# A two-layer hybrid decoder trunk: TensorE's wait before it reuses an accumulator counts finished tiles instead of first sums

## What is computed

```python
for i in range(2):
    h = rms_norm(x, norm_mix_pre[i])
    z = h @ w_in[i]                        # 2048 x 6400
    y_r = rwkv7_mix(token_shift(z[:, :3328]), ...)   # 16 heads of 64, delta-rule state
    y_a = moba_attention(rope(q), rope(k), v)        # 8 heads of 128
    y = concatenate([y_r, y_a]) @ w_out[i]           # 2048 x 2048
    x = x + rms_norm(y, norm_mix_post[i])
    h = rms_norm(x, norm_mlp_pre[i])
    m = square(relu(h @ w_up[i])) @ w_down[i]        # 2048 x 8192, 8192 x 2048
    x = x + rms_norm(m, norm_mlp_post[i])
```

## Time and profile before

| | |
|---|---|
| median of 3 runs | 2776.0 us (2775.13 to 2776.6) |
| the profiled execution | 2776.0 us, of which the span of the engines' work is 2774.3 us |
| PE busy | 97% of the span |
| DVE busy | 64% |
| ACT busy | 44% |
| POOL busy | 9% |
| mean granted TensorE clock | 0.988 of full speed |

### The profile page before, as it was taken

How to read it: one execution, slowest core, us unless ns; L and a number is a source line. 1 busy time by engine, 2 the same in 40 slices (tenths; PEclk the granted TensorE clock), 3 DMA queues, 4 the chain that set the end, 5 groups by cost and what they waited for, 6 DMA issues and landing times.

```text
span 2774.3 us, 50423 instructions
## 1 busy us (share of the span) xinstructions
PE 2682.2 (97%) x16787; PEld 2197.0 (79%) x16787; DVE 1775.2 (64%) x2961; ACT 1219.9 (44%) x1976; POOL 244.9 (9%) x341
## 2 busy tenths in 40 slices
PE   7999999999999999999989999999999999999998
PEld 6777777777888888888877777777778888888886
DVE  5777776655756656556577777777566566565565
ACT  5444443345544434444454444444454344444443
POOL 3211111100000000000012222221000000000000
PEclk9999999999999999999999999999999999999999
DMA  6333333345566565565633333332455665555654
GB/s 196 97 93 93 101 99 100 93 141 170 182 198 189 188 192 180 196 188 189 190 112 102 100 100 93 100 93 94 158 169 187 198 187 190 183 188 198 188 186 155
DMA packets 438043, 420.25 MB, mean 151 GB/s; under 512 B 19518, under 2 KB 351952, under 8 KB 437968
## 3 DMA queue, kind: packets, MB, share of 16 engines
q1 hardware_dynamic: 434320, 412.75, 47.5%
q0 software_dynamic: 3648, 6.52, 0.9%
HBM read 417.10 MB, written 2.10 MB: 151 GB/s over the span
## 4 chain that ended last, share of the span: by engine, by line
PE 90%; DVE 6%; issue 1%; ACT 1%; DMA 0%; DVEq 0%; POOL 0%; SPq 0%; ACTq 0%; POOLq 0%
PE gemm_bank L516 29%; PE gemm_bank L517 15%; PE gemm_bank L541 11%; PE gemm_bank L543 10%; PE gemm_bank L542 10%; PE gemm_bank L519 2%; PE mix_bank L696 2%; DVE b_zt L1157 1%; PE mix_bank L708 1%; PE mix_bank L705 1%; PE mix_bank L660 1%; DVE b_rn L1251 1%; PE mix_bank L726 1%; PE mix_bank L730 1%; PE mix_bank L740 1%
## 5 line engine op out<-in xcount | busy, mean ns | idle before, releaser
L516 PE MATMUL gemm_bank<-b_hT,b_whi 128*128 128x512 f32 x3420 | 1282.6, 413 | 13.6 <-DVE b_wlo L1148 10.0
L1148 DVE TENSOR_TENSOR b_wlo<-b_raw,b_whi 128x1024 fp32r<-128x1024 f32 x745 | 906.2, 1229 | 530.5 <-ACT b_whi L890 528.8
L890 ACT ACTIVATE b_whi<-b_raw 128x1024 fp32r<-128x1024 f32 x777 | 810.1, 1057 | 605.3 <-PE gemm_bank L543 422.1
L517 PE MATMUL gemm_bank<-b_hT,b_wlo 128*128 128x256 f32 x3648 | 1020.7, 284 | 0.0
L516 PEld LDWEIGHTS gemm_bank<-b_hT,b_whi 128*128 128x128 f32 x3420 | 650.9, 190 | 183.5 <-issue 29.8
L517 PEld LDWEIGHTS gemm_bank<-b_hT,b_wlo 128*128 128x128 f32 x3648 | 698.1, 191 | 15.0 <-issue 5.3
L541 PE MATMUL gemm_bank<-b_whi,b_mT 128*128 128x512 f32 x1280 | 502.8, 393 | 0.0
L543 PE MATMUL gemm_bank<-b_whi,b_mT 128*128 128x512 f32 x1280 | 498.3, 389 | 0.0
L542 PE MATMUL gemm_bank<-b_wlo,b_mT 128*128 128x512 f32 x1280 | 498.2, 389 | 0.0
L541 PEld LDWEIGHTS gemm_bank<-b_whi,b_mT 128*128 128x128 f32 x1280 | 240.2, 188 | 51.4 <-issue 1.8
L543 PEld LDWEIGHTS gemm_bank<-b_whi,b_mT 128*128 128x128 f32 x1280 | 240.2, 188 | 50.1
(11 more groups left out here) (239 smaller groups left out, 2301.2 us busy)
## 6 DMA issues: line engine op xcount, KB each, us to landing
b_raw<-in_w_up SPq DMA_DIRECT2D x256, 512.0 KB
b_raw<-in_w_down SPq DMA_DIRECT2D x256, 512.0 KB
b_raw<-in_w_in SPq DMA_DIRECT2D x384, 256.0 KB
b_raw<-in_w_out SPq DMA_DIRECT2D x60, 512.0 KB
b_raw<-in_w_in SPq DMA_DIRECT2D x8, 512.0 KB
b_xt<-in_x SPq DMA_DIRECT2D x4, 512.0 KB, 6.0
b_raw<-in_w_out SPq DMA_DIRECT2D x8, 256.0 KB
out<-b_xt SPq DMA_DIRECT2D x8, 256.0 KB, 2.3
```

What stands on the lines that cost most here:

```text
L516: mm(bank[b0 + b][:, :], whi[r][:, cols], pair, start=first, stop=False)
L517: m = mm(bank[b0 + b][:, 0:SEQ], wlo[r][:, cols], act[:, kt, 0, :], start=False, stop=False)
L890: f(whi[r][:, :], raw[r][:, :, :].rearrange("p a b -> p (a b)"), ACT.Copy).then_inc(hi_done, 1)
L1148: tt(wlo[r][:, :], flat(raw[r][:, :, :]), whi[r][:, :].bitcast(F32), ALU.subtract).then_inc(lo_done, 1)
```

## The change

Three waits of PE name another semaphore, with the same counts. PE may now reuse a bank only when the whole tile has been finished, and not as soon as its sum has been taken out of the bank. No computation, order of work, buffer or DMA is changed.

```diff
@@ -524,7 +524,7 @@ def group(k, d, tiles, act, b0, after={})
                 if not (isinstance(tiles, int) and tiles <= 0):
-                    pe.wait_ge(raw_sum, tiles)
+                    pe.wait_ge(tile_out, tiles)
@@ -589,7 +589,7 @@ def pair_ticks(a, b, k, d, tiles)
                     if kt == 0:
-                        pe.wait_ge(raw_sum, tiles + 2 * (g == 2))
+                        pe.wait_ge(tile_out, tiles + 2 * (g == 2))
```

## The result

The changed kernel took 2796.65 us (median of 4 runs, 2793.1 to 2799.0) beside 2776.3 us for the kernel before (4 runs); the ratio is 1.0072, with a 95% interval of 1.0055 to 1.0087. The forecast was 2787 us, with a range of 2781 to 2796: the direction was right, the forecast rise was half of what came, and the time lies 0.65 us above the range. The profiled execution took 2794.85 us, with a span of 2793.2.

A forecast was written before the change was run, and what follows sets the result against it. The prediction took PE to bound the kernel (90% of the chain). Leftover waiting and more low-clock stretches in the mixers, plus 0.7 for layer 1's first group, summed to +10.7, say +11, on 2776.0: 2787 us, range 2781 to 2796.

The forecast's parts named there:

- the fill slides over the wait at L639: Mixer start: first fill slides 3.27 us, 2.7 vanish in PE's wait at L639, 0.57 us are left in layer 0.
- 7 x 0.57 in layer 0: Mixers 0 to 6: each pays in full the 0.57 us of fill slide left after L639's wait.
- The first fill starts 0.25 us behind the second multiply: Mixer 2 start: multiply ends at 200.72, fill starts at 200.97, the same 0.25 us as behind the adds before.
- Layer 1's first group costs 0.7: Start of layer 1: PE waits for two multiplies ending 0.68 us behind the adds, with nothing covering it.
- no other wait costs anything: MLP, later mixer groups, output projection: a whole group between drain and reuse covers the wait, 7.2 us in the MLP.
- I take a fall in 5 of the 6 long mixers 1 to 6: Joined gaps of 3.56 us in layer 0 drop PE's clock toward 1.2 GHz in five mixers, where four fell before.
- rival 1: All mixers: every gap brings the clock down, 2794 us, or 2799 with low stretches twice as long in four; chance 0.15.
- The price of 1.33 us: Mixer start to start: 67.50 us with a low-clock stretch against 66.17 without; about 1.25 in layer 1.
- Mixer 7 gets faster by 0.6 us: Mixer 7: fill slides inside its 4.0 us gap, low clock meets the fill and partly ends sooner; -0.6, between -1.3 and 0.
- Rival 2: Mixers: the waits lengthen but the clock falls no oftener, 2782 us; chance 0.12.
- rival 3: Mixers: fill, L639 and next ticks run without a gap, so the clock stops falling, 2772.6 us; chance 0.05.
- Rival 4: First fill: multiplies end before PE's LoRA products or the slide fits L639's wait, nothing seen, 2776 to 2777 us; chance 0.05.

The follow-up runs named there:

- 13 / 11 unused matmuls: Changed kernel plus 13 (layer 0) or 11 (layer 1) matmuls with unused results ahead of each mixer's LoRA products: 2784.32 us, 10.1 more than the kernel before.

## Why the prediction was right and wrong, point by point

- *A wait that PE gains is paid in full, unless it would have waited a little later anyway; the fill slides over the wait at L639.* Right. PE's wait moved from L1265 to L1157, 51.3 us where I said some 45, and L639's wait is gone. By itself this costs 4.3 us, measured with no low stretch in either kernel; my terms for it, 7 x 0.57 in layer 0, nothing in layer 1 and 0.7 for its first group, give 4.7.
- *The first fill starts 0.25 us behind the second multiply.* Right: 200.85 + 3.38 = 204.23, and L516 at 204.49.
- *Layer 1's first group costs 0.7, and no other wait costs anything.* Right: everything but the first fill gave 1.5 us, of which 0.7 is that wait, and the stretch with the MLP grew by 0.6.
- ***I take a fall in 5 of the 6 long mixers 1 to 6 and in 4 of the 6 mixers 9 to 14; half a fall each in mixers 0 and 8; a fall costs 1.33 us.*** This step failed, as a mis-sized term. Its mechanism, a longer idle piece and with it more low clock, was right and has been shown by keeping PE busy. But every mixer had a fall, all of 1 to 6 and 9 to 14 and also 0, 8 and 15, and seven of them lasted 6.8 us and not 3.4. The low clock grew from 27 to 78 us. Divided as the measurement is, the forecast gave 10.7 - 4.7 = 6.0 us to the clock; it measured 16.0. The count came from six rows with gaps of 2.6 us and one with 4.0, and the kernels with 13 / 11 unused matmuls show how little such a count holds: 10 falls where the rows of about 2 us gave at most six. That a low stretch could be of double length I had only in rival 1.
- *The price of 1.33 us* for a fall of 3.4 us was about right in layer 0: 6.55 us against 5.0 for the 28 matmuls of the fill in mixer 2, so 1.55, and 1.5 from start to start on the mean of mixers 2, 4 and 6. A double one costs 2.2, and the sum has no term for it.
- *Mixer 7 gets faster by 0.6 us.* Not seen by itself. Its stretch has 0.77, a double fall.
- *Rival 1, every gap brings the clock down, 2794, or 2799 with twice the length in four mixers.* This is what happened. I gave it 0.15. The Trainium skill's rule against idle gaps between bursts ("TensorE: Matmul & The Clock Gate", the section on why this matters for your kernels) was the better guide here than my count of rows. The changed kernel's trace agrees with it in all sixteen mixers. Without exception, as the rival has it, it doesn't hold: of the fourteen mixers with gaps of about 2.1 and 1.5 us, four had no fall. Double falls came in seven mixers, not in four, at about 0.75 us more each.
- *Rival 2*, no more falls, and *rival 3*, no falls, are both refuted by the sixteen falls; but 2771.34 us is what rival 3 gives (2772.6), and it was reached once the idle time was filled. *Rival 4*, hidden anyway, falls with the 3.59 us of waiting.
- *The range* ended at 2796, between rival 1 and its own extension to 2799. It should have reached the latter.

## What to carry to other kernels

A wait on a semaphore that means "finished" where "read out" is enough costs little in waiting if PE waits soon after anyway, but it can join two short idle pieces into one long one. The bill then comes as slower matmuls behind the gap, in no list of waits: look at the granted clock in the stretch behind it, and compare the time per matmul. To tell the two apart, fill the gap with matmuls that nobody needs; if that stretch's granted clock rises and the time falls, it was the clock. And before real work is moved into a gap, ask what holds its end: here it was POOL's two splits beside DVE's instructions, so that work saved on PE came back as a longer multiply.

## What the runs showed of the hardware that I hadn't expected

- Eighteen unused matmuls of 256 columns in each gap of 2.5 us (fourteen in layer 1, where it was 2.0) made a kernel 8.0 us faster (2767.07 against 2775.08).
- With a gap of 3.6 us, the clock stayed at the low level for 6.8 us in some mixers, where it fell inside the gap, and for 3.4 us in others, where it fell when PE was busy again; with gaps of 2.1 and 1.5 us it was 3.4 us in each of ten.
- DVE's second multiply at L1157, with both inputs in SBUF, took 2.6 us beside POOL's splits, and the pair 0.75 us without them. The scan at L1257, which also reads two tiles in SBUF, went from 0.70 to 2.93 us once it ran beside them. This agrees with the Trainium skill ("SBUF — State Buffer", the section on who interferes with whom): a DVE instruction with two inputs from SBUF contends with a POOL instruction that reads SBUF. The adds at L1154, with one input from PSUM, took 0.76 us for the pair beside the same splits.
- The changed kernel scattered over 6 us from run to run, and the kernel before over 2 to 5, with the same instructions and data; the changed kernel's run of 2799.0 us had a mean granted clock of 0.978 and its run of 2793.1 us one of 0.981.
